# Reordering the sum transfers of a Strassen-type FFN, and the order of its last job, in a one-core transformer step

## What is computed

```python
def swiglu(h, wg, wu, wd):
    return (jax.nn.silu(h @ wg) * (h @ wu)) @ wd
...
x = x + gate2 * swiglu(modulate(rmsnorm(x, g_ffn), shift2, scale2), w_gate, w_up, w_down)
```

## Time and profile before

| | us |
|---|---|
| three timed runs | 888.97, 889.58, 889.75; median 889.58 |
| the profiled execution's own time | 889.07 |
| span in its profile (first to last instruction) | 887.2 |
| PE busy | 875.1 |
| DVE busy | 707.3 |
| ACT busy | 467.4 |
| POOL busy | 122.3 |

### The profile page before, as it was taken

How to read it: one execution, slowest core, us unless ns; L and a number is a source line. 1 busy time by engine, 2 the same in 40 slices (tenths; PEclk the granted TensorE clock), 3 DMA queues, 4 the chain that set the end, 5 groups by cost and what they waited for, 6 DMA issues and landing times. The chain is left out here.

```text
span 887.2 us, 16538 instructions
## 1 busy us (share of the span) xinstructions
PE 875.1 (99%) x6227; PEld 832.4 (94%) x6227; DVE 707.3 (80%) x1331; ACT 467.4 (53%) x973; POOL 122.3 (14%) x155
## 2 busy tenths in 40 slices
PE   7999999999999999999999999999999999999998
PEld 5788888898989999999999999999999999999997
DVE  5567898899788499774777879997777898777887
ACT  6563444777777533432246645555544555545553
POOL 0000000010000000000000033313423322333221
PEclk9999999999999999999999999999999999999999
DMA  9964343541543220238307289868999886898867
GB/s 367 368 219 171 129 146 120 165 128 52 169 152 107 72 72 1 85 107 325 126 24 238 65 186 205 178 168 204 196 201 194 177 189 167 199 210 189 182 151 147
DMA packets 51663, 145.32 MB, mean 164 GB/s; under 512 B 6000, under 2 KB 12416, under 8 KB 50176
## 3 DMA queue, kind: packets, MB, share of 16 engines
q1 hardware_dynamic: 32000, 102.38, 35.0%
q0 software_dynamic: 18864, 41.11, 24.0%
q10 hardware_dynamic: 720, 0.77, 0.2%
HBM read 121.68 MB, written 12.20 MB: 151 GB/s over the span
## 5 line engine op out<-in xcount | busy, mean ns | idle before, releaser
L1320 ACT ACTIVATE w_hi<-stage 128x512 fp32r<-128x512 f32 (+1 forms) x186 | 105.7, 608 | 93.2 <-DMA stage<-stage 48.0
L2013 DVE TENSOR_TENSOR w_lo<-stage,w_hi 128x512 fp32r<-128x512 f32 (+1 forms) x186 | 117.7, 667 | 20.4 <-ACT w_hi L1320 20.0
L2628 PE MATMUL ps<-m_hi,w_hi 128*128 128x320 f32 x304 | 93.9, 309 | 0.0
L2628 PE MATMUL ps<-m_lo,w_hi 128*128 128x320 f32 x304 | 93.9, 309 | 0.0
L2628 PE MATMUL ps<-m_hi,w_lo 128*128 128x320 f32 x304 | 93.9, 309 | 0.0
L1415 DVE TENSOR_TENSOR w_lo<-stage,w_hi 128x1024 fp32r<-128x1024 f32 x47 | 57.2, 1222 | 35.9 <-ACT w_hi L887 35.5
L2628 PE MATMUL ps<-h_hi,w_hi 128*128 128x320 f32 x272 | 84.1, 309 | 0.8 <-DVE w_lo L2013 0.8
L2628 PE MATMUL ps<-h_hi,w_lo 128*128 128x320 f32 x272 | 84.0, 309 | 0.0
L2628 PE MATMUL ps<-h_lo,w_hi 128*128 128x320 f32 x272 | 84.0, 309 | 0.0
L2628 PE MATMUL ps<-y_hi,w_hi 128*128 128x320 f32 x264 | 81.7, 309 | 0.0
L2628 PE MATMUL ps<-y_hi,w_lo 128*128 128x320 f32 x264 | 81.6, 309 | 0.0
(11 more groups left out here) (317 smaller groups left out, 2437.0 us busy)
## 6 DMA issues: line engine op xcount, KB each, us to landing
stage<-w_main SPq DMA_DIRECT2D x118, 512.0 KB, 4.2
x<-w_ada SPq DMA_DIRECT2D x21, 512.0 KB, 4.5
stage<-stage POOLq DMA_DIRECT2D x38, 256.0 KB, 4.7
qk<-w_ada SPq DMA_DIRECT2D x7, 1024.0 KB, 13.8
scr<-w_main POOLq DMA_DIRECT2D x28, 256.0 KB, 6.2
y_t<-scr POOLq DMA_DIRECT2D x22, 320.0 KB, 6.7
s_second<-w_main POOLq DMA_DIRECT2D x26, 256.0 KB, 6.1
stage<-w_main POOLq DMA_DIRECT2D x19, 256.0 KB, 6.4
```

The lines of the kernel that those rows point to most:

```text
L1320: act.activation(w_hi[:, slot, at:at + job_half(j) * P], left_stage(op, j), ACT.Copy).then_inc(left_hi[op], 1)
L2013: dve.tensor_tensor(w_lo[:, slot, w], left_stage(op, j), w_hi[:, slot, w].bitcast(F32), ALU.subtract).then_inc(left_lo[op], 1)
L2628: ins = pe.matmul(ps[:, BANK_OF[op], 0:TH], wt[:, slot, w], right(op, part, j, k), start=k == 0 and n == 0, stop=k == half - 1 and n == 2)
```

## The change

Three edits. (a) On POOL, `s4(j + 1)` is issued ahead of `s1(j + 2)`, in the 16 places where both exist; at the start, S3's second term of job 0 and S1 and S3's first term of job 1 go ahead of S2 of job 0. (b) At job 0 ACT and DVE split A11 of job 1 earlier. (c) In the last job ACT copies the first product ahead of scaling job 29's second tile, and VectorE calls `last_tile` for each term as it comes, in place of forming c21's and c22's sums first.

```diff
@@ POOL @@
             s3_first(0)
-            s2(0)
             s3_second_term(0)
-            s4(0)
             s1(1)
             s3_first(1)
+            s2(0)
             s3_second_term(1)
+            s4(0)
             for j in range(len(JOBS)):
...
                 if j + 2 < len(JOBS):
                     s3_first(j + 2)
+                if by_transfers(j + 1):
+                    s4(j + 1)
                 if by_transfers(j + 2):
                     s1(j + 2)
-                if by_transfers(j + 1):
-                    s4(j + 1)
                 if j + 2 < len(JOBS):
                     s3_second_term(j + 2)
@@ ACT @@
             def copy_p1(j):
                 act.wait_ge(left_used["A11"], nth(j))
-                if j and JOBS[j - 1][1] is not None:
+                if j == len(JOBS) - 1:
+                    act.wait_ge(v_done, nth(j - 1))
+                elif j and JOBS[j - 1][1] is not None:
...
+                if not j:
+                    left_high("A11", 1)
+                if not more:
+                    copy_p1(j)
                 if ended is not None:
                     y_high(ended)
                 else:
...
-                copy_p1(j)
+                if more:
+                    copy_p1(j)
@@ DVE @@
-            def last_tile(second, src, cols):
+            def last_tile(second, src, cols, last=ALU.add):
...
                 dve.wait_ge(rest_in, 32)
                 dve.wait_ge(ada_dve, N_ADA2)
-                dve.wait_ge(c12_done, nth(len(JOBS) - 1))
...
+                if not more:
+                    dve.wait_ge(c11_done, nth(j))
+                    last_tile(0, high_sb, slice(0, TH))
+                    dve.wait_ge(r_done, 2 * down_number(j))
                 if own_sums:
                     s4(j + 1)
                 else:
                     u2_v(j)
+                if not more:
+                    dve.wait_ge(v_done, nth(j))
+                    own.mark(last_tile(1, low_sb, slice(0, TH)))
                 c12(j)
...
-                else:
-                    last_tile(0, high_sb, slice(0, T)).then_inc(last_done, 1)
-                c22_u3(j)
+                if more:
+                    c22_u3(j)
 
             j = len(JOBS) - 1
+            dve.wait_ge(c12_done, nth(j))
+            last_tile(0, high_sb, slice(TH, T)).then_inc(last_done, 1)
+            c22(j)
             dve.wait_ge(c22_done, nth(j))
             last_tile(1, low_sb, slice(TH, T)).then_inc(last_done, 1)
-            own.mark(last_tile(1, low_sb, slice(0, TH)))
+            own.wait()
+            own.mark(last_tile(1, of_product("S3"), slice(0, TH), ALU.subtract))
             dve.wait_ge(left_used["A22"], nth(j))
             own.wait()
-            last_tile(1, of_product("A22"), slice(0, TH)).then_inc(last_done, 1)
+            last_tile(1, of_product("A22"), slice(0, TH), ALU.subtract).then_inc(last_done, 1)
```

More of the change, by code:

```diff
@@ L1382, in _ @@
                     y_sums_high(ended)
-                if more:
+                if j and more:
                     left_high("A11", j + 1)
@@ L2062, in c21, with c22 @@
                 dve.tensor_tensor(by_half[:, H_C21, :], of_product("A22"), by_half[:, H_U, :], ALU.add).then_inc(c21_done, 1)
-            def last_tile(second, src, cols):
+            def c22(j):
+                dve.wait_ge(left_used["S3"], nth(j))
+                dve.wait_ge(v_done, nth(j))
+                dve.tensor_tensor(by_half[:, H_C22, :], by_half[:, H_V, :], of_product("S3"), ALU.subtract).then_inc(c22_done, 1)
+            def last_tile(second, src, cols, last=ALU.add):
                 n, dst = KT - 2 + second, kept[2 + second]
@@ L2073, in last_tile @@
                         ins = dve.scalar_tensor_tensor(out=dst[:, t], in0=src[:, t], scalar=mod[:, g + kind:g + kind + 1],
-                                                       in1=dst[:, t], op0=ALU.mult, op1=ALU.add)
+                                                       in1=dst[:, t], op0=ALU.mult, op1=last)
                 return ins
@@ L2114, in _ @@
                 own_sums = more and sums_by_vector(j + 1)
+                if not j:
+                    left_low("A11", 1)
                 if starts_down(j):
```

## The result

The changed kernel took 890.25 us (median of 22 runs, 888.01 to 893.94), the kernel before 889.18 us beside it (22 runs, 888.42 to 891.04): ratio 1.0013, interval 1.0007 to 1.0019. So it is slower by about 1.1 us, where 0.3 us less was forecast. The second measurement shows no difference; the loss is small, but in neither is there a gain. What follows asks where a wait of 0.92 us that did go away went to, and what the tail cost.

A forecast was written before the change was run, and what follows sets the result against it. TensorE was taken as the bound, busy 875.1 of 887.2 us, with one 0.92 us wait and DVE's chain at the end. -0.92 + 0.64 = -0.28 us took the median from 889.58 to 889.3 us, range 888.0 to 891.2.

The forecast's parts named there:

- (a) at the start: Job 1's S4 transfer: issued about 521 to 523, so PE's wait for w_lo near 532 goes, 0.92 us gained.
- (a) later: S1 behind S4 in 16 places: next S2 up to 0.9 us later, taken as nothing, range 0 to some 2 us.
- The ring: POOL's loop of S2, S4 and S1 transfers: 13.0 us a turn, where PE needs 12.3 us per job.
- rival 1: Transfers become a ring longer than a job, S2 slips 0.7 us per job: 896.6 us in full, chance 0.09.
- a later issue need not mean a later landing: S2's transfer usually lands behind SP's unit load issued with it, an argument for taking nothing for the later transfers.
- rival 1 in its mild form: S2 late in two or three jobs about job 17: costs 0.5 to 2 us, 890 to 891, chance 0.14.
- (b): Job 0 on ACT and DVE, A11 of job 1 split earlier: DVE's later idle time takes it up, nothing.
- (c): Last job: c11 1.22 us earlier, but the first last_tile waits for rest_in, so the end comes 0.64 us later.
- other bound: Last job without a wait for rest_in: DVE's chain ends at 884.32, 0.6 us gained; not taken.
- The sum: Whole kernel: -0.92 at job 1 plus 0.64 in the tail gives -0.28 us, median 889.3 us.

The follow-up runs named there:

- second measurement: The changed kernel measured once more later, on another chip: 890.44 us against 889.80 us for the kernel before, ratio 1.0000.
- ring_longer: The changed kernel with S1's transfer one place later still, behind S3's second term: 13.5 us over the kernel before.
- tail_only: The kernel before with the changed last job alone, transfers as before: 2.7 us over the kernel before.
- old_order_later: The changed kernel with S4 ahead of S1 only for job 1, the old order from job 2 on: 889.37 us.
- after_again: The changed kernel once more, unaltered: its profiled execution took 889.15 us, and the median is 1.3 us above that.
- transfers_only: The kernel before with the new transfer order and earlier A11 of job 1, its own tail kept: 0.1 us under the kernel before.
- rest_split: The changed kernel with the two reloads counted apart, so the first last_tile waits for its own row alone: 1.2 us under the kernel before.
- reload_before_add: The changed kernel with job 29's first result added only once both reloads have landed: the time went up by 2 us.

## Why the prediction failed, step by step

**(a) at the start was right.** S4 of job 1 was issued at 522.12 (521 to 523 predicted), 5.20 us behind S2's where it had been 7.23, and the wait is gone in all eleven profiled executions with the new start, `ring_longer` among them.

**(a) later is the step that failed**: "I take nothing for this part, with a range from 0 to some 2 us." The ring is there. In the changed kernel POOL's waits from 512 us on read

```profile
POOL stage L836 <- DMA stage<-w_main: 83.9, 16, 6.0
```

where before they read

```profile
POOL stage L836 <- DVE w_lo L2013: 70.4, 18, 5.4
```

so S2 now waits for S1's landing where it waited for a split. One turn in POOL's timeline is 655.25 - 642.93 = 12.32 us, PE's own step (12.3):

```profile
642.93 0.87 POOL L836 DMA_DIRECT2D stage<-stage  x1 [5.82 <-DMA stage<-w_main]
...
647.19 0.87 POOL L842 DMA_DIRECT2D stage<-stage  x1 [2.82 <-DMA stage<-stage]
647.74 1.21 POOL L819 DMA_DIRECT2D stage<-w_main  x1
...
655.25 0.88 POOL L836 DMA_DIRECT2D stage<-stage  x1 [5.39 <-DMA stage<-w_main]
```

Its terms: S1's landing 7.0 us in the median (6.2 taken, from the row of S3's transfers; the page before has 6.4 for S1's own, `stage<-w_main`), S2 to S4 4.26 us here (5.86 taken). The first makes the ring 0.8 us longer, the second 1.6 shorter. With the 0.55 and 0.4 us of the prediction that is 12.2 us, not rival 1's 13.0, so the ring just meets PE's step and does not slip in every job. The second is the argument "a later issue need not mean a later landing", and the view of line L836 in 540:880 bears it out. First the kernel before:

```profile
L836 POOL DMA_DIRECT2D stage<-stage x17: 865/875/893, 543.2 to 837.9; - x17
...
DMA to landing us min/median/max: 4.7/5.3/7.0
```

and the changed kernel:

```profile
L836 POOL DMA_DIRECT2D stage<-stage x17: 865/875/893, 544.0 to 840.8; - x17
...
DMA to landing us min/median/max: 3.4/4.0/6.2
```

From the Trainium skill's rule (DMA: Bandwidth & Descriptors, "Queues, rings and completion order") that each DMA engine goes round between its queues a packet at a time, I had drawn that a later issue is a later landing in full. That is not in the rule, and it would have given 896.6 us; the 4.0 against 5.3 us say otherwise. S1, issued 1.1 us behind S2 before and now behind S4, is no longer under way beside S2, and that may be the reason; no run tests it alone.

What failed is the price of the remainder, put at nothing. The kernels with the new order to the end lost 0.71, 0.09, 1.43, 0.92, 1.84 and 1.68 us, 1.1 in the mean; those with the new start and the old order later 0.09, 0.39, 0.09 and 0.09, 0.2 in the mean. So the new order costs about 0.9 us on these means, as much as job 1's wait had (1.10, 1.03 and 0.42 lost in three kernels with the old start, 0.85 in the mean). The net of (a) is then some +0.3, not -0.92, an estimate from six and three executions that scatter by more than that. This is rival 1 in its mild form (0.5 to 2 us, 890 to 891), to which I gave 0.14. I had found the right buffer (the gap of `c21`) and one of the two jobs, 17, but looked for slack at S4's and S2's splits alone. What PE waits for is `y_lo`, further back on DVE's queue, and mostly in job 27, where I had not looked.

**(b)** cost nothing, as taken: nowhere does PE wait in job 0 or 1.

**(c)** came out at its size in the two profiled executions of the changed kernel: 0.64 us predicted, 0.64 and 0.71 measured (tails of 2.60 and 2.67 against 1.97). That it is so exact in the first is luck: the load took 3.6 us, not 3.2, and the first `last_tile` began 3.05 us before PE's end, not 3.31, while the chain from there took 5.65 us, not 5.92. The "other bound", without the wait, was 1.36 us of tail by my chain and 1.21 by measurement. But the sentence "second load is issued at 876.39 and takes 3.2 us" took the landing for fixed. From SP's and POOL's timelines and the view of L785:

```
kernel               load issued  add issued  add after load by  landed in
tail_only            877.29       877.11      -0.18              5.8
old_order_later      876.00       876.03      +0.03              4.9
after_again          875.80       875.97      +0.17              3.5
before               876.39       876.60      +0.21              3.2
transfers_only       876.93       877.17      +0.24              4.2
changed              876.67       877.00      +0.33              3.6
rest_split           876.31       876.87      +0.56              3.1
ring_longer          889.86       888.87      -0.99              4.5
reload_before_add    876.99       881.02      +4.03              3.4
```

Behind the adding transfer or within 0.03 us of it, it takes 4.5 to 5.8 us; ahead of it 3.1 to 4.2. These are nine executions, one of each kernel, and no run varies this order alone, so the adding transfer as the cause is likely and not shown. The kernel before asked for the row only at 881.24, 1.65 us after it had landed, and that cover hid this. The changed kernel has none, so the tail follows the landing. That this happens to the changed kernel in some executions is argued from its spread, not shown: both its profiles have the quick landing.

**The sum.** -0.28 as forecast, with (a) at +0.3 in place of -0.92, gives +0.9 us; measured were +1.1 and +0.6 by the medians. The timed parts divide it in another way: the transfers alone came out 0.1 us under before, where 0.92 was forecast, and the tail alone 2.7 over, where 0.64 was. The parts make more than the whole, so each of the two terms was too hopeful, and how the loss of the changed kernel's median divides between the ring and the load's landing stays open.

## What to carry to other kernels

Before moving a transfer on a queue, close the loop: add up issue, landing and the next issue over one turn, and compare it with TensorE's step; a sum within a us of that step isn't free, and the place that pays may stand well behind the split that is late. Before an instruction is moved forward, list what it waits for and how much cover each wait had, since a load that was never late may be the next bound, and its landing isn't a constant. Here the fix was two things together: the load issued some 15 us sooner, and S4 ahead of S1 in job 1 alone.

## What the runs showed of the hardware that I had not expected

A transfer's landing differs by more than its size would tell. The same 256 KB (S2's sum, `stage<-stage`) landed in a median of 5.3 us before, with S1's transfer issued some 1.1 us behind it, in 4.0 us in the changed kernel, where S1's goes out behind S4's, and in 3.3 us in `ring_longer`, where it goes out later still. The same 320 KB reload took 3.1 to 5.8 us at the end of the program, by where it stood beside an adding transfer, and 6.8 to 8.8 us in the kernels that issue it at about 860, where it has time to spare. A 160 KB store took 1.8 us, and 3.5 us in `reload_before_add`, under two adding transfers. Which neighbour does how much is not separated by these runs.
